# Four array quarters for the backward direction and a turned T in the RWKV chunk stages

## The chip, the core and the metric

The kernel runs on one core of a Trainium2 chip. The metric is the device time of the whole kernel in microseconds, as a median of several runs; less is better. TensorE is called PE here, VectorE DVE, ScalarE ACT, GpSimd POOL.

## What is computed

One trunk layer of a hybrid backbone: 512 latent and 128 context tokens, width 1024. The change touches one part, the RWKV-7 scan in both directions over time, for 8 heads of width 64:

```python
def step(s, inp):
    r_t, w_t, k_t, v_t, kk_t, a_t = inp
    sa = jnp.einsum("bhvk,bhk->bhv", s, -kk_t)
    s = (s * w_t[:, :, None, :] + sa[..., None] * (kk_t * a_t)[:, :, None, :]
         + v_t[..., None] * k_t[:, :, None, :])
    return s, jnp.einsum("bhvk,bhk->bhv", s, r_t)
for d, reverse in enumerate((False, True)):
    ...
    y, s_fin = _wkv7_scan(rh, w, kd, vh, kk, a, s0[:, d].astype(f32), reverse)
```

The rest (modulated norms, input projection, attention, gated merge, MLP) is dense work on PE and is the same in both kernels.

## The kernel before

The scan is done in chunks of 64 tokens (`CH`). Within a chunk the recurrence is a triangular system, so the kernel needs the inverse of a 64 by 64 unit triangular matrix for each chunk, direction and head. It builds that inverse by doubling the solved block size, in levels.

Two heads make a head pair: one head lies in partitions 0 to 63, the other in 64 to 127. The function `chunks(it)` runs twice (`it` 0 and 1), the "half" of the text, and each half works on two head pairs `s` = 0 and 1. A half takes five groups `g`; a group holds, for each pair, two directions `d` and two chunks `q`, so eight 64 by 64 problems of one pair are handled by one "stage". Stages are named by two letters:

- KB and KA (L853): products of bt and of kt with ar, 64 by 128 each. AB and AK on DVE mask them into `abm` and `akm`.
- R0 and T0 (DVE): the first level of the inverse `rm` and its transpose `tm`.
- for levels l = 1 to 5: H_l (PE, L873) multiplies `abm` with `tm`; ACT copies the result from PSUM to `hm` (L1488); G_l (PE, L885) multiplies `hm` with `rm`; C_l (DVE, L1877) copies the blocks of that level into `tm`; V_l (DVE, L1881) transposes `tm` back into `rm`. After G5 comes V5 (L1873), the last copy into `rm`.
- TR (L865): bt and kt turned, copied by ACT to `bkt`.
- P, U, S, Y for q = 0 and 1: right side, solution (`rm` times `pw`), new state, output. ACT copies P and U out, DVE scales the state (S, L1892), ACT or DVE moves Y out. These are LAGGED: in round r they work on group r - 1, while the H and G stages work on group r.

No scheduler is involved. The lists `PE_ST`, `DV_ST` and `AC_ST` are the order of the stages in one round for each engine; `paired` issues each stage for s = 0 and then for s = 1. Each engine works its list strictly in order, and a stage starts with waits on counters of the stages that it needs. In the second half ACT and DVE also have pieces of the next phase between these stages (`between_stages`: splitting the attention output, L1459 and L1916, and a weight block).

A float32 matmul shows in the trace as two records, so one H stage of one pair is 16 records: 2 directions, 2 chunks, 2 heads, 2 records. A matmul of head 0 reads partitions 0 to 63 and writes partitions 0 to 63, one of head 1 reads and writes 64 to 127. This is the matter of the change: of the four quarters of the array (input half by output half) two are used.

## Time and profile before

| | |
|---|---|
| median of 3 runs | 1368.11 us (1368.07 to 1368.47) |
| the profiled execution, its own time | 1369.97 us |
| its span, first to last instruction | 1368.2 us |
| mean granted PE clock | 0.983 |
| PE busy | 1289.2 us, 94% |
| DVE busy | 689.7 us, 50% |
| ACT busy | 550.7 us, 40% |
| first half of the chunk stages | 321.5 to 446.0 us |
| second half | 587.6 to 707.9 us |

Busy time is the union of the records of an engine. A PE record lasts until its result has landed, so that neighbours overlap: a PE that shows as busy can still be waiting for short times between stages.

### The profile page before, as it was taken

To read this page: it belongs to the slowest core of one execution; us is meant where nothing else is said; L and a number is where in the kernel's file an instruction comes from. 1 tells how busy PE (TensorE), PEld (TensorE's weight loads), DVE (VectorE), ACT (ScalarE), POOL (GpSimd) and SP (SyncE) were. 2 spreads that over 40 slices of the span, in tenths; PEclk is the share of its full clock that TensorE was granted. 3 is DMA by queue.
4 is the path that set the end of the run, shared out by engine and by line. 5 is a ranking of instruction groups with operands and counts; after the bars stand their busy time and mean duration, and the time that the engine had idled before them with its cause. 6 is when DMAs were issued, how large, how long until landed. Compare 5 with 4: busy or idle time off the path is not lost.

```text
span 1368.2 us, 31729 instructions
## 1 busy us (share of the span) xinstructions
PE 1289.2 (94%) x13903; PEld 1191.0 (87%) x13903; DVE 689.7 (50%) x1036; ACT 550.7 (40%) x864; POOL 42.2 (3%) x103
## 2 busy tenths in 40 slices
PE   4899999998999779999999999899999999999995
PEld 1899999998999554489989878799999999999995
DVE  3427742642544666565547512554554544533544
ACT  3635534432233577624342212733433334333433
POOL 0100011000010000000000000000000000000000
PEclk9899999999999999999999999999999999999998
DMA  9422265315000200010116495022121121022222
GB/s 389 147 72 101 100 267 183 119 49 210 9 5 4 93 1 1 0 54 4 39 42 230 172 376 185 10 87 89 61 92 61 63 90 38 23 77 73 72 71 93
DMA packets 24027, 131.70 MB, mean 96 GB/s; under 512 B 2896, under 2 KB 3664, under 8 KB 15344
## 3 DMA queue, kind: packets, MB, share of 16 engines
q1 hardware_dynamic: 19104, 103.98, 21.7%
q0 software_dynamic: 4816, 26.11, 5.1%
q8 instruction: 90, 1.47, 0.5%
q14 instruction: 17, 0.14, 0.0%
HBM read 111.74 MB, written 18.34 MB: 95 GB/s over the span
## 4 chain that ended last, share of the span: by engine, by line
PE 58%; DVE 4%; ACT 3%; DMA 1%; issue 1%; DVEq 0%; ACTq 0%
PE ps L715 29%; PE ps L1230 11%; PE ps L885 2%; PE ps L873 2%; PE ps L1096 2%; PE ps L853 1%; PE ps L740 1%; PE ps L759 1%; DMA adl<-in_wada 1%; DVE nmax L1995 1%; PE ps L750 1%; PE ps L1002 1%; PE ps L1072 1%; PE ps L865 1%; PE ps L1043 1%
## 5 line engine op out<-in xcount | busy, mean ns | idle before, releaser
L715 PE MATMUL ps<-h2lo,whi 128*128 128x322 f32 x672 | 154.5, 311 | 0.7 <-ACT facc L1332 0.7
L715 PE MATMUL ps<-h2hi,wlo 128*128 128x322 f32 x672 | 155.0, 312 | 0.0
L715 PE MATMUL ps<-h2hi,whi 128*128 128x322 f32 x672 | 154.0, 310 | 0.0
L1685 DVE TENSOR_TENSOR wlo<-raw,whi 128x2048 fp32r<-128x2048 f32 x47 | 107.5, 2288 | 75.1 <-ACT whi L1293 75.1
L715 PE MATMUL ps<-hlo,whi 128*128 128x322 f32 x544 | 127.9, 316 | 1.0 <-ACT qkv L1358 1.0
L715 PE MATMUL ps<-hhi,wlo 128*128 128x322 f32 x544 | 125.4, 312 | 0.0
L715 PE MATMUL ps<-hhi,whi 128*128 128x322 f32 x544 | 124.7, 310 | 0.0
L715 PEld LDWEIGHTS ps<-h2hi,whi 128*128 128x128 f32 x672 | 114.2, 190 | 0.0
L715 PEld LDWEIGHTS ps<-h2lo,whi 128*128 128x128 f32 x672 | 113.0, 189 | 0.9 <-DVE wlo L1685 0.9
L715 PEld LDWEIGHTS ps<-h2hi,wlo 128*128 128x128 f32 x672 | 113.7, 189 | 0.0
L1732 DVE SCALAR_TENSOR_TENSOR facc<-fraw,par,facc 128x642 f32<-128x642 f32 x44 | 39.0, 887 | 137.3 <-ACT facc L1332 137.3
L1331 ACT ACTIVATE fraw<-ps 128x644 f32<-128x644 f32 x44 | 31.2, 710 | 181.4 <-PE ps L715 180.1
L1293 ACT ACTIVATE whi<-raw 128x2048 fp32r<-128x2048 f32 x47 | 90.0, 1915 | 17.3 <-PE ps L715 11.8
L715 PEld LDWEIGHTS ps<-hlo,whi 128*128 128x128 f32 x544 | 91.4, 189 | 4.2 <-issue 2.4
L715 PEld LDWEIGHTS ps<-hhi,whi 128*128 128x128 f32 x544 | 92.4, 190 | 0.0
L715 PEld LDWEIGHTS ps<-hhi,wlo 128*128 128x128 f32 x544 | 91.9, 189 | 0.0
L1230 PE MATMUL ps<-dlo,whi 128*128 128x322 f32 x344 | 79.3, 312 | 3.2 <-DVE dlo L2149 2.1
L1230 PE MATMUL ps<-dhi,wlo 128*128 128x322 f32 x344 | 79.5, 313 | 0.0
L1230 PE MATMUL ps<-dhi,whi 128*128 128x322 f32 x344 | 78.5, 309 | 0.0
L2148 DVE TENSOR_TENSOR wlo<-raw,whi 128x512 fp32r<-128x512 f32 x44 | 30.4, 692 | 84.2 <-ACT dhi L1631 84.2
L1877 DVE COPY_PREDICATED tm<-con,ps 128x256 f32<-128x256 int32 x80 | 35.6, 445 | 65.9 <-PE ps L885 65.0
L1630 ACT ACTIVATE whi<-raw 128x512 fp32r<-128x512 f32 x44 | 27.8, 633 | 95.0 <-PE ps L1230 93.0
(353 smaller groups left out, 2592.7 us busy)
## 6 DMA issues: line engine op xcount, KB each, us to landing
raw<-in_wblk SPq DMA_DIRECT2D x48, 1024.0 KB, 4.9
adl<-in_wada SPq DMA_DIRECT2D x8, 2048.0 KB, 8.1
raw<-in_wdn SPq DMA_DIRECT2D x44, 256.0 KB, 2.6
adaw<-in_wada SPq DMA_DIRECT2D x4, 2048.0 KB, 20.3
gate_scratch<-gout POOLq DMA_DIRECT2D x16, 322.0 KB, 2.5
gld<-gate_scratch POOLq DMA_DIRECT2D x8, 644.0 KB, 4.6
attention_inputs_used<-attention_scratch SPq DMA_DIRECT2D x1, 5056.0 KB, 15.4
u_scratch<-uout POOLq DMA_DIRECT2D x12, 320.0 KB, 2.4
```

Source lines behind the costliest of these rows:

```text
L715: mm = pe.matmul(o, w, v, start=first, stop=last and w is hi and x is xh[n])
L873: mm = pe.matmul(bank(b1, CH, CH * (2 * d + q))[r], abm[s][g % 2][r, d, q, 0, :], tm[s][r, d, q, :], start=True, stop=True)
L885: mm = pe.matmul(bank(b0, CH, CH * (2 * d + q))[r], left, right, start=True, stop=True)
L1096: mm = pe.matmul(bank(4 + u % 2)[64 * p:64 * p + 64], vo_u[:, c, u // 2, 64:128], pt[p][:, c, :], start=c == 0, stop=c == 5)
L1230: mm = pe.matmul(o, w, v, start=(k == 0 and q == 0), stop=(k == FF - 1 and q == 2))
L1293: ac.activation(whi[s][:, :], raw[s][:, :], ACT.Copy).then_inc(hi_done, 1)
L1331: ac.activation(fr[j][:, :], tile(2 * j), ACT.Copy)
L1630: ac.activation(whi[0][:, 512:1024] if second else whi[s][:, 0:512], raw[s][:, 0:512], ACT.Copy)
L1685: TT(wlo[s][:, :], raw[s][:, :], whi[s][:, :].bitcast(F32), ALU.subtract).then_inc(lo_done, 1)
L1732: st.last(STT(fa[j][:, 1:TP - 1], fr[j][:, 0:TP - 2], taps(0), fa[j][:, 1:TP - 1], ALU.mult, ALU.add))
L1877: ins = dv.copy_predicated(t1[:, :, :, :], lev[:, l - 1].unsqueeze(2).broadcast_to(each), steps_of(bank(b0, 4 * CH)))
L2148: TT(wl, raw[s][:, 0:512], wh.bitcast(F32), ALU.subtract)
```

## The change

Five things are done. (1) The backward direction (d = 1) writes its products H, P and U into the other half of the output partitions (`away`), and reads them there in G and U; so d = 0 uses two quarters of the array and d = 1 the other two. The two directions write to two PSUM banks, and ACT and DVE read two banks in one instruction. (2) H now also multiplies `tm` with the identity, which turns it; ACT copies both results to `hr`, and G takes both operands from there. V1 to V4 on DVE go; T0 and the V5 copy stay. H5 turns T into `rm` with an ACT copy of its own. (3) KA moves from behind KB to the end of the round, AK with it. (4) The lists of stages are written anew. (5) PE gets its stages from `staggered`: pair 0 runs one stage ahead of pair 1. DVE and ACT keep `paired`.

```diff
@@ -322,16 +323,15 @@
             for s in range(2):
                 made[s].insert(0, sb(f"{name}{s}_{g}", [P, 2, 2, 2, CH]))
         if g:
-            tm = [sb(f"tm{s}", [P, 2, 2, CH]) for s in range(2)]
-            hm = [sb(f"hm{s}", [P, 2, 2, CH]) for s in range(2)]
+            hr = [sb(f"hr{s}", [P, 2, 2, 2, CH]) for s in range(2)]
             assert spot[0] == ring_half
...
-    PE_ST = ["KB", "KA", "P0", "H1", "U0", "G1", "S0", "Y0", "H2", "G2", "P1", "H3", "U1", "G3", "S1", "Y1", "H4", "G4",
-             "TR", "H5", "G5"]
-    DV_ST = ["AB", "R0", "T0", "AK", "C1", "V1", "S0", "C2", "V2", "C3", "V3", "S1", "Y1", "C4", "V4", "V5"]
-    AC_ST = ["P0", "H1", "U0", "H2", "P1", "H3", "U1", "Y1", "H4", "TR", "H5"]
+    PE_ST = ["KB", "P0", "U0", "S0", "H1", "Y0", "G1", "H2", "P1", "G2", "U1", "H3", "S1", "G3", "H4", "Y1", "G4", "H5", "TR",
+             "G5", "KA"]
+    DV_ST = ["AB", "R0", "T0", "S0", "C1", "C2", "S1", "C3", "Y1", "C4", "V5", "AK"]
+    AC_ST = ["P0", "U0", "H1", "H2", "P1", "U1", "H3", "H4", "Y1", "H5", "TR"]
...
+    def staggered(names):
+
+        stages = list(in_order(names))
+        first = [(g, name, 0) for g, name in stages]
+        second = [(g, name, 1) for g, name in stages]
+        out = [first[0], second[0], first[1]]
+        for a, b in zip(first[2:], second[1:]):
+            out += [a, b]
+        return out + [second[-1]]
...
             if name in ("KB", "KA"):
-                if g == 0:
+                if name == "KA":
+                    ac("H5")
+                elif g == 0:
                     pe.wait_ge(dv_prep, 10 * it + 10)
-                elif name == "KA":
+                else:
                     dv("V5", g - 1)
-                else:
-                    ac("H5", g - 1)
-                b, src = (b1, bt[s]) if name == "KB" else (b0, kt[s])
+                b, src = (b0, bt[s]) if name == "KB" else (b1, kt[s])
...
             elif name[0] == "H":
                 l = int(name[1])
                 dv("T0" if l == 1 else f"C{l - 1}")
-                for d in range(2):
+                for turn in range(2):
                     for q in range(2):
-                        for r in half:
-                            mm = pe.matmul(bank(b1, CH, CH * (2 * d + q))[r], abm[s][g % 2][r, d, q, 0, :], tm[s][r, d, q, :],
-                                           start=True, stop=True)
+                        for d in range(2):
+                            for r, away in zip(half, half[::-1]):
+                                left, right = (tm[s][r, d, q, :], ident[r, r]) if turn else \
+                                    (abm[s][g % 2][r, d, q, 0, :], tm[s][r, d, q, :])
+                                mm = pe.matmul(bank(b0 + d, CH, CH * (2 * turn + q))[away if d else r], left, right,
+                                               start=True, stop=True)
             elif name[0] == "G":
                 l = int(name[1])
                 ac(f"H{l}")
-                dv("AK" if l == 1 else f"V{l - 1}")
-                for d in range(2):
-                    for q in range(2):
-                        for r in half:
-                            left, right = rm[s][g % 2][r, d, q, :], hm[s][r, d, q, :]
+                for q in range(2):
+                    for d in range(2):
+                        for r, away in zip(half, half[::-1]):
+                            at = away if d else r
                             if l == 5:
-                                left, right = right, left
-                            mm = pe.matmul(bank(b0, CH, CH * (2 * d + q))[r], left, right, start=True, stop=True)
+                                mm = pe.matmul(bank(b0, CH, 4 * CH + CH * (2 * d + q))[at], hr[s][at, d, 0, q, :],
+                                               rm[s][g % 2][at, d, q, :], start=True, stop=True)
+                            else:
+                                mm = pe.matmul(bank(b0 + d, CH, 4 * CH + CH * q)[r], hr[s][at, d, 1, q, :],
+                                               hr[s][at, d, 0, q, :], start=True, stop=True)
             elif name[0] == "P":
                 if q == 0:
                     ac("TR")
+                    dv("AK")
+                    if g > 0:
+                        if g - 1 in ADDED:
+                            dv("Y1", g - 1)
+                        else:
+                            ac("Y1", g - 1)
                     if g == 1:
                         pe.wait_ge(sl_done, it + 1)
                     elif g > 1:
                         dv("S1", g - 1)
                 else:
                     dv("S0")
-                for d in range(2):
-                    for r in half:
-                        mm = pe.matmul(bank(b2, CH, CH * d)[r], akm[s][g % 2][r, d, q, 0, :], vt64[s][r, chunk_of(g, d, q), :],
-                                       start=True, stop=first)
-                    if not first:
-                        for r in half:
-                            mm = pe.matmul(bank(b2, CH, CH * d)[r], ar[s][r, d, chunk_of(g, d, q), 0, :], state(q)[r, d, :],
-                                           start=False, stop=True)
+                    if g == NG - 1:
+                        pe.wait_ge(pe_g[s], at_stage(PE_ST, it, g, "Y0"))
+                for n in range(1 if first else 2):
+                    for d in range(2):
+                        for r, away in zip(half, half[::-1]):
+                            left, right = (ar[s][r, d, chunk_of(g, d, q), 0, :], state(q)[r, d, :]) if n else \
+                                (akm[s][g % 2][r, d, q, 0, :], vt64[s][r, chunk_of(g, d, q), :])
+                            mm = pe.matmul(bank(b2 + d, CH, 6 * CH)[away if d else r], left, right, start=n == 0,
+                                           stop=first or n == 1)
...
                 for d in range(2):
-                    for r in half:
-                        mm = pe.matmul(bank(b2, CH, P + CH * d)[r], rm[s][g % 2][r, d, q, :], pw[s][r, d, :], start=True, stop=True)
+                    for r, away in zip(half, half[::-1]):
+                        at = away if d else r
+                        mm = pe.matmul(bank(b2 + d, CH, 7 * CH)[r], rm[s][g % 2][at, d, q, :], pw[s][at, d, :], start=True,
+                                       stop=True)
...
-                if q == 0 and g > 0:
-                    if g - 1 in ADDED:
-                        dv("Y1", g - 1)
-                    else:
-                        ac("Y1", g - 1)
...
-            for g, name, s in paired(PE_ST):
+            for g, name, s in staggered(PE_ST):
...
                 if name[0] == "H":
-                    ins = ac.activation(hm[s][:, :, :, :].rearrange("p d q n -> p (d q n)"), bank(b1, 4 * CH), ACT.Copy)
+                    if name == "H5":
+                        ac.activation(hr[s][:, :, 0, :, :].rearrange("p d q n -> p d (q n)"), ps[:, b0:b0 + 2, 0:2 * CH], ACT.Copy)
+                        ins = ac.activation(rm[s][g % 2][:, :, :, :].rearrange("p d q n -> p d (q n)"),
+                                            ps[:, b0:b0 + 2, 2 * CH:4 * CH], ACT.Copy)
+                    else:
+                        ins = ac.activation(hr[s][:, :, :, :, :].rearrange("p d m q n -> p d (m q n)"),
+                                            ps[:, b0:b0 + 2, 0:4 * CH], ACT.Copy)
                 elif name[0] in "PU":
-                    dst, at = (pw[s], 0) if name[0] == "P" else (uw[s], P)
-                    ins = ac.activation(dst[:, :, :].rearrange("p d n -> p (d n)"), bank(b2, P, at), ACT.Copy)
+                    dst, at = (pw[s], 6 * CH) if name[0] == "P" else (uw[s], 7 * CH)
+                    ins = ac.activation(dst[:, :, :], ps[:, b2:b2 + 2, at:at + CH], ACT.Copy)
...
-                ins = dv.copy_predicated(r1[:, :, :, :], last.unsqueeze(2).broadcast_to(each), steps_of(bank(b0, 4 * CH)))
+                ins = dv.copy_predicated(r1[:, :, :, :], last.unsqueeze(2).broadcast_to(each), steps_of(bank(b0, 4 * CH, 4 * CH)))
...
-                ins = dv.copy_predicated(t1[:, :, :, :], lev[:, l - 1].unsqueeze(2).broadcast_to(each), steps_of(bank(b0, 4 * CH)))
-            elif name == "T0" or name[0] == "V":
-                mine("R0" if name == "T0" else "C" + name[1])
-                src, dst = (r1, t1) if name == "T0" else (t1, r1)
-                ins = dv.transpose(dst[:, :, :, :].rearrange("p d q n -> p (d q n)"), src[:, :, :, :].rearrange("p d q n -> p (d q n)"))
+                ins = dv.copy_predicated(t1[:, :, :, :], lev[:, l - 1].unsqueeze(2).broadcast_to(each),
+                                         ps[:, b0:b0 + 2, 4 * CH:6 * CH].rearrange("p d (q n) -> p d q n", q=2))
+            elif name == "T0":
+                mine("R0")
+                ins = dv.transpose(t1[:, :, :, :].rearrange("p d q n -> p (d q n)"), r1[:, :, :, :].rearrange("p d q n -> p (d q n)"))
...
-            if name in ("V2", "V4") and 1 <= g <= 3:
-                lows(2 * g - 2 + (name == "V4"))
+            if name in ("C2", "C4") and 1 <= g <= 3:
+                lows(2 * g - 2 + (name == "C4"))
```

On PE, first where the third level meets the state stage, in the middle of a round. L909 is U, L885 is G, L916 to L920 are S; buffers 191 and 192 belong to pair 0 and pair 1. Before:

```order
L909 MATMUL ps<-pw_191,rm_0_185 64x64 x4
L909 MATMUL ps<-pw_192,rm_0_187 64x64 x4
L885 MATMUL ps<-hm_177,rm_1_186 64x64 x8
L885 MATMUL ps<-hm_178,rm_1_188 64x64 x8
L916 MATMUL ps<-si_1_196,con 64x64 x2
L918 MATMUL ps<-vt_0_189,bkt_0_183 64x64 x2
L920 MATMUL ps<-uw_193,bkt_0_183 64x64 x2
```

Of the change (L886 is H with its turn, L899 is G, L940 to L944 are S, hr_177 is pair 0, tm_190 pair 1):

```order
L886 MATMUL ps<-tm_190,abm_0_182 64x64 x8
L886 MATMUL ps<-con,tm_190 64x64 x8
L899 MATMUL ps<-hr_177 64x64 x8
L940 MATMUL ps<-si_1_200,con 64x64 x2
L942 MATMUL ps<-vt_1_192,bkt_1_176 64x64 x2
L944 MATMUL ps<-uw_196,bkt_1_176 64x64 x2
...
L886 MATMUL ps<-tm_189,abm_0_181 64x64 x8
L886 MATMUL ps<-con,tm_189 64x64 x8
```

Before, G3 of both pairs is followed by S1 of both; now S1 of pair 1 stands behind G3 of pair 0.

The same place on DVE. L1877 is C, L1881 is V, L1892 is the scaling of the state (si_0_195 of pair 0, si_0_197 of pair 1). Before, C3, V3, the state of q = 1, C4:

```order
L1877 COPY_PREDICATED tm_175<-con,ps 128x256
L1877 COPY_PREDICATED tm_176<-con,ps 128x256
L1881 STREAM_TRANSPOSE rm_0_185<-tm_175 128x256
L1881 STREAM_TRANSPOSE rm_0_187<-tm_176 128x256
L1892 TENSOR_TENSOR si_0_195<-ps,ex_144 128x128
L1892 TENSOR_TENSOR si_0_197<-ps,ex_145 128x128
L1877 COPY_PREDICATED tm_175<-con,ps 128x256
L1877 COPY_PREDICATED tm_176<-con,ps 128x256
```

Of the change (L1902 is C, L1917 the state), from C2 to C4:

```order
L1902 COPY_PREDICATED tm_189<-con,ps 128x256
L1902 COPY_PREDICATED tm_190<-con,ps 128x256
L1917 TENSOR_TENSOR si_0_197<-ps,ex_144 128x128
L1917 TENSOR_TENSOR si_0_199<-ps,ex_145 128x128
L1902 COPY_PREDICATED tm_189<-con,ps 128x256
L1902 COPY_PREDICATED tm_190<-con,ps 128x256
L1902 COPY_PREDICATED tm_189<-con,ps 128x256
L1902 COPY_PREDICATED tm_190<-con,ps 128x256
```

The transposes are gone, and the state of both pairs now stands ahead of C3 of pair 0 where it stood behind C3 and V3.

## Rows read from the trace of the kernel before

**Rows 1.** Head of the page: the span.

```profile
span 1368.2 us, 31729 instructions
```

**Rows 2.** Windows: us, then PE, PEld, DVE, ACT, POOL busy, PEclk, DMA, GB/s.

```profile
321.50:343.20 21.70, 17.89 (x449) 16.33 (x450) 10.52 (x25) 5.74 (x13) 2.02 (x5) 0.96 0.88 316
...
587.60:604.60 17.00, 16.63 (x455) 15.29 (x450) 10.27 (x25) 5.63 (x13) 1.38 (x4) 1.00 0.21 86
604.60:627.10 22.50, 22.44 (x696) 22.03 (x694) 13.97 (x37) 8.70 (x26) 0.75 (x2) 1.00 0.02 4
627.10:650.90 23.80, 23.75 (x742) 23.34 (x740) 13.46 (x35) 8.97 (x26) 0.75 (x2) 1.00 0.05 9
650.90:676.00 25.10, 24.01 (x745) 23.46 (x742) 13.41 (x33) 8.79 (x24) 0.75 (x2) 1.00 0.13 46
676.00:707.90 31.90, 31.79 (x983) 30.85 (x979) 15.53 (x38) 10.87 (x30) 0.10 (x1) 1.00 0.02 5
```

**Rows 3.** Groups of PE instructions by form in 587.6 to 707.9.

```profile
L873 PE MATMUL ps<-tm,abm 64*64 64x64 f32 x800 | 27.8, 219 | 0.3
L885 PE MATMUL ps<-hm,rm 64*64 64x64 f32 x640 | 22.6, 220 | 0.2
...
L897 PE MATMUL ps<-vt,akm 64*64 64x64 f32 x160 | 9.7, 218 | 1.0 <-issue 1.0
...
L853 PE MATMUL ps<-ar,bt 64*64 64x128 f32 x160 | 9.6, 269 | 0.0
...
L901 PE MATMUL ps<-si,ar 64*64 64x64 f32 x128 | 8.0, 218 | 0.0
L909 PE MATMUL ps<-pw,rm 64*64 64x64 f32 x160 | 6.9, 220 | 0.0
L885 PE MATMUL ps<-rm,hm 64*64 64x64 f32 x160 | 5.7, 221 | 0.2
```

**Rows 4.** Timeline of one level, all engines.

```profile
384.18 1.10 PE L873 MATMUL ps<-tm,abm 64*64 64x64 f32 x32
...
384.86 0.85 ACT L1488 ACTIVATE hm<-ps 128x256 f32<-128x256 f32 x2
...
385.29 1.15 PE L885 MATMUL ps<-hm,rm 64*64 64x64 f32 x32
386.02 0.91 DVE L1877 COPY_PREDICATED tm<-con,ps 128x256 f32<-128x256 int32 x2 [2.74 <-PE ps L885]
...
386.27 0.28 PE L865 MATMUL ps<-con,bt 64*64 64x64 f32 x4
```

**Rows 5.** Groups of ACT and of DVE by form, 587.6 to 707.9.

```profile
L1488 ACT ACTIVATE hm<-ps 128x256 f32<-128x256 f32 x50 | 19.2, 384 | 30.7 <-PE ps L873 28.5
L1493 ACT ACTIVATE bkt<-ps 128x512 f32<-128x512 f32 x10 | 6.0, 597 | 8.2 <-PE ps L865 8.2
L1491 ACT ACTIVATE pw<-ps 128x128 f32<-128x128 f32 x20 | 5.5, 278 | 28.1 <-PE ps L901 23.6 <-PE ps L897 4.5
...
L1459 ACT ACTIVATE branch_hi<-raw 128x512 fp32r<-128x512 f32 x4 | 2.5, 623 | 0.0
...
L1877 DVE COPY_PREDICATED tm<-con,ps 128x256 f32<-128x256 int32 x40 | 17.8, 445 | 31.9 <-PE ps L885 31.4
L1881 DVE STREAM_TRANSPOSE rm<-tm 128x256 f32<-128x256 f32 x40 | 15.3, 420 | 0.0
...
L1892 DVE TENSOR_TENSOR si<-ps,ex 128x128 f32<-128x128 f32 x14 | 3.8, 275 | 3.3 <-PE ps L920 2.5
```

**Rows 6.** Modulation blocks, four column groups: by form; one whole; its first four.

```profile
L750 PE MATMUL ps<-adl,silu_c 128*32 128x512 f32 x128 | 15.4, 598 | 1.6 <-DMA adl<-in_wada 1.6
...
781.56 1.92 PE L750 MATMUL ps<-adl,silu_c 128*32 128x512 f32 x16
...
781.56 0.64 PE L750 MATMUL ps<-adl,silu_c 128*32 128x512 f32 x4
```

**Rows 7.** Timeline of PE behind a gap, then a window behind it.

```profile
340.45 1.03 PE L873 MATMUL ps<-tm,abm 64*64 64x64 f32 x28 [2.67 <-issue]
...
341.40:344.90 3.50, 3.48 (x52) 3.41 (x50) 0.89 (x2) 0.43 (x2) 0.00 (x0) 0.51 0.11 30
```

More of the change, by code:

```diff
@@ L301, in build @@
     stv = [w[:, 3 * P:4 * P].rearrange("p (d n) -> p d n", d=2) for w in hpw]
+    smid = [sb(f"smid{s}", [P, 2, CH]) for s in range(2)]
     assert spot[0] <= keep_u, (spot[0], keep_u)
@@ L329, in build @@
         rm[s] += [sb(f"rm{s}_{g}", [P, 2, 2, CH]) for g in range(2)]
+    tm = [sb(f"tm{s}", [P, 2, 2, CH]) for s in range(2)]
     vt64 = [sb(f"vt64_{s}", [P, NC, CH]) for s in range(2)]
@@ L333, in build @@
     si = [[sb(f"si{s}_{n}", [P, 2, CH]) for n in range(2)] for s in range(2)]
-    smid = [sb(f"smid{s}", [P, 2, CH]) for s in range(2)]
     ysum = [sb(f"ysum{s}", [P, NT, P]) for s in range(2)]
@@ L1863, in chunk_stage @@
             if name in ("AB", "AK"):
-                b, dst = (b1, abm[s]) if name == "AB" else (b0, akm[s])
+                b, dst = (b0, abm[s]) if name == "AB" else (b1, akm[s])
                 product("KB" if name == "AB" else "KA")
@@ L1869, in chunk_stage @@
                 dv.wait_ge(po_g[s], at_stage(PO_ST, it, g, "R0"))
-                ins = dv.copy_predicated(r1[:, :, :, :], near.unsqueeze(2).broadcast_to(each), steps_of(bank(b1))[:, :, :, 0:CH])
+                ins = dv.copy_predicated(r1[:, :, :, :], near.unsqueeze(2).broadcast_to(each), steps_of(bank(b0))[:, :, :, 0:CH])
             elif name == "V5":
                 product("G5")
-                ins = dv.copy_predicated(r1[:, :, :, :], last.unsqueeze(2).broadcast_to(each), steps_of(bank(b0, 4 * CH)))
+                ins = dv.copy_predicated(r1[:, :, :, :], last.unsqueeze(2).broadcast_to(each), steps_of(bank(b0, 4 * CH, 4 * CH)))
             elif name[0] == "C":
```

## Prediction

> **What bounds the kernel now.** I read the windows first. The chunk stages take 321.5 to 446.0 us and 587.6 to 707.9 us; nothing that the diff touches lies elsewhere, so of the span of 1368.2 us [rows 1] some 245 us are in play. In the windows of the second half, cut at each KB, PE is busy in nearly all of every round: 17.0, 22.5, 23.8, 25.1 and 31.9 us, the fourth with a PE gap of 1.1 us; DVE has 10 to 15 us of work in them and ACT 6 to 11 [rows 2]. A PE record outlives its place in the queue, so "busy" has to be turned into a pace. In the timeline of a level the 32 records of an H stage of both pairs last 1.10 us, of which 0.22 is the last record's way out, so a record takes 0.029 us of PE's time and an H stage of one pair 0.47; the G stages take the same [rows 3, 4]. The 64x128 products take 9.6 us for 160 with five such tails, so 0.056 each [rows 3]. A half has 3264 records of the first kind (H 800, G 800, P 304, U 160, and TR, S and Y, which stay) and 320 of the second: 95.0 + 17.9 = 112.9 us of work. The second half takes 120.3 us, so PE waits some 7.4 us in it, the gap included. PE's work is the bound, and the waits are small.
>
> The same timeline gives the delays from engine to engine. H starts at 384.18, its first copy on ACT at 384.86, that is 0.47 for the stage and 0.21 behind it; the copies end so that G starts at 385.29, 0.05 behind the first of them; C follows at 386.02, again 0.21 behind the G stage when 0.05 for the restart of PE are counted [rows 4].
>
> **What the quarters give.** H gets twice the records (1600), four at a time instead of two. G1 to G4 (640 records), P (304) and U (160) keep their number and go four at a time; G5, KB, KA, TR, S and Y are as before. If four quarters run at once, four records take the 0.058 us of two. H then costs what it did, G saves 640 x 0.0146 = 9.3 us, P 4.4, U 2.3: 16.0 us a half.
>
> No row of this trace shows four 64x64 quarters. The nearest one are the modulation blocks, where the output is cut into four column groups: 128 records of 598 ns take 15.4 us in all, a block of 16 takes 1.92 us, and its first four lie within 0.64 us, so they start within 0.04 us of each other [rows 6]. So four parts of the array work at once and four starts are no obstacle; I take four. The bound from the other side is no gain at all over two (the pace of rows 3): H costs 23.3 us more a half, the others as before.
>
> The Trainium skill says otherwise: "TensorE: Matmul & The Clock Gate", in the section on the gap of 56 ns, has a floor of about 25 ns from start to start, however small the matmul. The trace speaks against it, by the four starts within 0.04 us [rows 6]. By the skill's floor a quarter's record would cost 0.025 us, and the 2704 of them in a half 28 us more than I take: the rival "few quarters" below.
>
> **What the new order costs.** I walk each round through the three lists with these durations: H 0.47 a pair, G 0.23, U 0.12, P 0.23; ACT's copy of H has 512 columns instead of 256, so 0.60 (the bkt copy) instead of 0.38; P and U copies 0.28, C 0.445, state 0.275 [rows 5]; an engine's next instruction can start some 0.09 before the last one's end. A stage starts when its queue has come to it and its inputs are there. Waits of PE in one half:
>
> - First round, nothing lagged. Before, a level takes 0.47 + 0.21 + 0.38 + 0.10 + 0.47 + 0.21 + 0.445 + 0.10 = 2.4 us. Now the copy is 0.22 longer and G 0.23 shorter: 2.4 again, with less work in it. PE waits 6.5 us (2.5 before).
> - Each of the four rounds with lagged work: S0 of pair 0 waits 0.80, because ACT takes P0 of both pairs before U0 of pair 0, and PE now issues P0 of pair 1 behind U0 of pair 0. H2 of pair 1 waits 0.55 for G1 and C1. U1 of pair 0 waits 0.66, the same crossing on ACT. H4 of pair 0 waits 0.96: on DVE the state of pair 1 now stands ahead of C3 of pair 0, and on PE S1 of pair 1 stands behind G3 of pair 0. Small ones 0.4. Together 3.4 us a round (0.8 before), 13.6 for four.
> - DVE adds the output of groups 0 and 3 (Y1) ahead of C4: 1.5 and 1.1 us before H5; and 0.8 in small waits in the second round.
> - The last round's lagged stages alone: AK now comes at the end, P0 waits 1.35 and 0.88 for it, S0 0.80, Y1 0.80 and 0.61: 4.4 us (1.1 before).
>
> That is 6.5 + 13.6 + 3.4 + 4.4 = 27.9 us against 7.3 us when the kernel before is walked in the same way (112.9 + 7.3 = 120.2; the trace has 120.3). So the first half changes by 27.9 - 7.3 - 16.0 = +4.6 us. In the second half ACT splits the attention output behind H2 and H4 of pair 1, 0.62 + 0.30 us [rows 5] or 0.73; before, this lay in ACT's idle time. Now P1's copy is queued behind it and U1 waits for that: 0.84, 0.84 and 0.64 more, and H5 0.7 more: +3.0. Second half +7.6 us.
>
> The V transposes (40 of 0.42 us a half [rows 5]) I cost at nothing: DVE is not what PE waits for there, G had its `rm` before ACT had `hm`. The buffer moves cost nothing either; no wait changes by them.
>
> **Sum.** 4.6 + 7.6 = +12.2 us, on the profiled execution (1368.2 us of span, 1.8 of time around it, 1369.97) and so on the median of 1368.1: 1380.3. PE's waits make one more half-speed window in the first rounds likely: there is one now, at 341.4 us, granted 0.51, behind a gap of 2.67 us in which PE waited for no engine [rows 7]; that round takes 21.7 us instead of 17.0 [rows 2]. PE will be at work for 12.0 of 18.5 us in a first round. I add 1 us for it. Predicted: 1381 us.
>
> **The rivals.**
>
> 1. The crossings overlap (faster). The four large waits of a lagged round (0.80, 0.55, 0.66, 0.96 = 3.0 us) rest on exact places in three queues; eight rounds hold 24 us. If they all vanish because the stages ahead of them finish a little sooner, the time is 1357. It decides at half of them, 12 us. For it: DVE loses 40 transposes of 0.42 us a half [rows 5], so its queue is emptier than the walk's worst places need. Against it: each is a queue's order, not a load, and each stage behind it is 0.23 to 0.6 long.
> 2. Few quarters (slower). With no more than two at once, the work is 136.2 us a half and the waits mostly disappear in it: about 160 a half, 1447 us. Rows 6 speak against it. An estimate by the Trainium skill's floor (the page named above), 125 us of work a half, would give about 150 a half and 1428 us.
> 3. Clock and instructions (slower). Every first round and every last round falls to the lower of PE's two levels, 1.2 instead of 2.4 GHz, for part of its length. The one case in the trace cost at most the 4.7 us by which the two first rounds differ, a gap of PE's own in it [rows 2, 7]; three more such would give 1381 + 14 = 1395. A half also has 3200 more PE instructions of 0.0146 us or less, so gaps "issue" like those at 340.45 would come more often.
> 4. No change: the waits grow by just what the quarters give, 1368.
>
> **How the numbers follow.** The forecast (with partly overlapping waits, 1372 to 1392) has a chance of 0.6; rival 1 0.17, spread from 1350 to 1367; rival 2 0.07; rival 3 0.12; no change 0.04. A measurement of this kernel tells about 0.2% (2.7 us) from no change. Faster by more: 0.18 (rival 1 and a little of the rest); within: 0.05; slower: 0.77. The range leaves out rival 2 and the ends of rivals 1 and 3: 1357 to 1399.
>
> **What would show it.** In the profile of the changed kernel: H with its turn should take 0.47 us a pair (32 records that last 0.7), G 16 records in some 0.45 with its tail; if H takes 0.93 the quarters don't overlap. Rounds from KB to KB of about 18.5, 24.2, 23.3, 23.3 us, and PE's busy share falling in them. ACT's H copy at 0.60. In the waits of PE, H on tm (DVE) and U and S on pw and uw (ACT) should lead, where now they hardly appear. Wrong would make me: H waits for C3 that don't come up because the state stage of pair 1 is done in time; or a last tail much shorter than 4 us.

## The result

The changed kernel takes 1417.35 us (median of 4 runs, 1414.47 to 1419.82) against 1368.29 for the kernel before beside it: 1.0348 times as long, 95% interval 1.0317 to 1.038. The forecast was 1381 us with a range of 1357 to 1399. The sign was right, the loss (49 us) four times as large as forecast (13), and outside the range.

The page of the changed kernel: the span, TensorE's busy time, and the queue that brings instructions (packets, MB).

```profile
span 1415.6 us, 34777 instructions
...
PE 1277.8 (90%) x15503; PEld 1171.3 (83%) x15503; DVE 662.7 (47%) x956; ACT 570.9 (40%) x884; POOL 43.4 (3%) x103
...
q8 instruction: 102, 1.67, 0.5%
```

The windows, cut at each KB as in [rows 2], with the first half above and the second below.

```profile
321.60:348.70 27.10, 17.15 (x595) 15.48 (x596) 6.71 (x15) 7.89 (x15) 2.01 (x5) 0.87 0.71 254
348.70:374.70 26.00, 21.62 (x854) 19.97 (x849) 9.68 (x24) 9.41 (x24) 0.80 (x2) 1.00 0.03 9
374.70:401.90 27.20, 22.55 (x902) 21.07 (x900) 9.19 (x22) 9.62 (x24) 0.80 (x2) 1.00 0.02 5
401.90:429.60 27.70, 22.52 (x907) 21.04 (x905) 9.21 (x22) 9.62 (x24) 4.34 (x4) 1.00 0.02 5
429.60:468.00 38.40, 30.10 (x1156) 27.96 (x1152) 12.66 (x30) 10.96 (x30) 0.00 (x0) 1.00 0.02 4
611.10:630.80 19.70, 15.02 (x597) 13.13 (x595) 6.72 (x15) 7.78 (x15) 1.33 (x4) 1.00 0.18 74
630.80:656.70 25.90, 21.02 (x856) 19.71 (x853) 11.26 (x28) 10.72 (x28) 1.07 (x2) 1.00 0.01 4
656.70:683.20 26.50, 22.29 (x903) 21.23 (x899) 10.87 (x26) 10.85 (x28) 1.07 (x2) 1.00 0.12 34
683.20:714.90 31.70, 24.03 (x906) 22.81 (x902) 10.72 (x24) 10.71 (x26) 1.21 (x2) 0.95 0.05 16
714.90:756.50 41.60, 32.33 (x1167) 29.18 (x1163) 15.00 (x33) 12.85 (x32) 1.06 (x2) 1.00 0.06 15
```

From the first record of the first KB to the start of the last record of Y, the halves take 146.4 and 143.2 us (124.4 and 120.2 before): +22.0 and +23.0, together nearly all of the 49. The excess over the forecast lies in every round and not in one accident: 27.1, 26.0, 27.2, 27.7 and 38.4 us in the first half, where 18.5, 24.2, 23.3 and 23.3 were forecast and some 35.5 were left for the last (120.2 + 4.6, less the four). The granted clock is 1.00 in eight of the ten windows (0.87 and 0.95 in the others), so it isn't the clock either. TensorE is busy for 22 of 27 us in a middle round, and idle in a kernel that it was said to bound.

What it waits for, in the waits of PE over the chunk stages of the second half (us in total, times, longest):

```profile
PE ps L886 <- DVE tm L1902: 6.8, 10, 1.7
PE ps L923 <- issue: 4.7, 6, 1.2
PE ps L886 <- issue: 3.5, 4, 1.5
PE ps L863 <- issue: 2.3, 1, 2.3
PE ps L940 <- ACT uw L1516: 2.3, 4, 0.6
PE ps L886 <- DVE tm L1906: 2.2, 2, 1.8
PE ps L875 <- issue: 2.2, 3, 1.1
PE ps L899 <- ACT hr L1512: 1.6, 4, 0.7
```

L886 is H, L923 P, L863 KB and KA, L940 the state, L899 G, L875 TR; L1902 is C and L1906 T0 on DVE. Half of the list is what the prediction had named: H on `tm`, the state on `uw`. The other half is "issue", TensorE idle while nothing that the profile shows holds it. All such rows of this view sum to 16.4 us in the first half and 14.9 in the second; in the kernel before they sum to 3.5 and 1.0. The view counts a halt from the modelled end of the last record, about 0.2 us behind its start, so it understates each. Not every such row is a halt without a cause: of the first half's 16.4 us, 1.9 are the two stages P0 of the last round (L923), which the new order makes wait for AK.

Where the halts fall is the finding. TensorE's timeline of the changed kernel, first around 407 us, then around 409 and 413:

```profile
406.90 0.46 PE L886 MATMUL ps<-tm,abm 64*64 64x64 f32 x16
407.18 0.41 PE L886 MATMUL ps<-con,tm 64*64 64x64 f32 x16
...
409.01 0.33 PE L886 MATMUL ps<-con,tm 64*64 64x64 f32 x7
409.54 0.34 PE L886 MATMUL ps<-con,tm 64*64 64x64 f32 x8 [0.20 <-issue]
...
412.18 0.46 PE L886 MATMUL ps<-tm,abm 64*64 64x64 f32 x16 [0.33 <-DVE tm L1902]
413.26 0.46 PE L886 MATMUL ps<-con,tm 64*64 64x64 f32 x16 [0.63 <-issue]
```

The first two rows are H and its turn as forecast: 16 records in 0.28 us, the next 16 about as fast, 0.47 us to the next stage's start. The stages at 409 and 413 break off inside, in the middle of the turn or between product and turn, where no instruction carries a wait. Counting TensorE's instructions (a record of a matmul and a record of a weight load are one each) gives their places. Below, worked out from the trace of the changed kernel, is each transfer of the instruction queue and each longer halt from 407 to 428 us that the profile calls "issue", with the number of instructions that PE had started by then. The first three halts lie inside a stage, the last three between two stages:

```
transfer 407.19 took 0.96
halt     409.12 -> 409.54  0.41   after instruction  9086
transfer 410.65 took 1.32
halt     412.42 -> 413.26  0.84   after instruction  9342
transfer 414.38 took 0.96
halt     416.01 -> 416.72  0.71   after instruction  9598
transfer 417.86 took 1.30
halt     420.02 -> 420.45  0.43   after instruction  9854
transfer 421.70 took 1.16
halt     423.12 -> 424.45  1.33   after instruction 10110
transfer 425.48 took 1.21
halt     427.48 -> 428.18  0.70   after instruction 10366
```

The numbers differ by exactly 256. The queue moved 1.67 MB in 102 packets, 16 KB each. The kernel before, with 3200 TensorE instructions fewer, has 90 packets, and a run with 6144 more than that (e4 below) has 114: 24 packets for 24 x 256 instructions. So a packet is a block of 256 instructions; TensorE runs out at the end of a block and goes on, in this stretch, 2.3 to 2.8 us after a transfer began. (The Trainium skill, "Advanced Engine Details and Errata", section on the ISA cache, has a line of 16 KB, 256 instructions. The halts and the packets agree. How many lines TensorE holds, no run here shows.) The changed kernel issues 8768 TensorE instructions in a half, the one before 7168.

The place can be followed through whole traces. When the semaphore instructions of PE's own sequencer, which are records too, are counted with the others, the numbers of all these halts leave the same remainder, 193, when divided by 256. In the halves of every run below, each "issue" halt of over 0.3 us from start to start is one of them, other than the stages P0 of the last round (the wait for AK) and a single one in e9. So the time lost at block ends can be summed for each run. The table has this in us for the two halves together (a halt is a step of over 0.1 us from one start to the next, less the 0.03 us of a usual one). "Rest" is the halves' time without it, "walked" what the prediction's way of walking the stages, which knows no supply, gave against before.

| run | halves | at block ends (halts) | rest | rest against before | walked |
|---|---|---|---|---|---|
| before | 244.5 | 5.2 (5) | 239.3 | | |
| changed | 289.6 | 36.2 (45) | 253.4 | +14.1 | +12.2 |
| e1, more instructions | 277.6 | 25.5 (40) | 252.1 | +12.8 | |
| e7, more small ones | 278.1 | 26.4 (38) | 251.7 | +12.4 | |
| e3, no turn | 246.7 | 7.6 (12) | 239.2 | -0.1 | -5 |
| e10, half of the turn | 273.9 | 23.2 (32) | 250.7 | +11.4 | |
| e2, pairs together | 281.7 | 42.3 (51) | 239.4 | +0.1 | -2 |
| e11, e10 and e2 | 257.0 | 22.3 (33) | 234.7 | -4.6 | |
| e9, lag alone | 275.0 | 2.7 (5) | 272.3 | +33.0 | +32 |
| e6, quarters alone | 235.9 | 14.7 (25) | 221.2 | -18.1 | -19 |
| e5, two quarters | 323.4 | 4.5 (3) | 318.9 | +79.6 | +79 |
| e8, state once | 267.8 | 3.9 (5) | 263.9 | +24.6 | |

Of the 45 us that the two halves grew, 31 are halts at block ends, and the other 14 are about what the walk forecast. A halt and a wait for a queue can cover each other, so this is a split of what the trace shows and not a proof that the two add.

### The profile page after: what moved, and what is told of

Its sections match the earlier page's. It is cut to its first block, busy times and chain, and to the rows that moved or that the text cites. A ratio compares the mean times of both kernels' runs of the same rounds, so it can differ in the third digit from the quotient of the medians.

```text
span 1415.6 us, 34777 instructions
## 1 busy us (share of the span) xinstructions
PE 1277.8 (90%) x15503; PEld 1171.3 (83%) x15503; DVE 662.7 (47%) x956; ACT 570.9 (40%) x884; POOL 43.4 (3%) x103
## 3 DMA queue, kind: packets, MB, share of 16 engines
q8 instruction: 102, 1.67, 0.5%
## 4 chain that ended last, share of the span: by engine, by line
PE 55%; DVE 4%; ACT 3%; issue 2%; DMA 1%; DVEq 0%; ACTq 0%
PE ps L725 28%; PE ps L1249 10%; PE ps L886 2%; PE ps L1115 2%; PE ps L863 1%; PE ps L750 1%; PE ps L769 1%; DMA adl<-in_wada 1%; DVE nmax L2020 1%; PE ps L760 1%; PE ps L1021 1%; PE ps L899 1%; PE ps L1091 1%; PE ps L875 1%; PE ps L1092 1%
## 5 line engine op out<-in xcount | busy, mean ns | idle before, releaser
L725 PE MATMUL ps<-hlo,whi 128*128 128x322 f32 x544 | 127.9, 316 | 1.0 <-ACT qkv L1377 1.0
L1512 ACT ACTIVATE hr<-ps 128x512 f32<-128x512 f32 x80 | 47.6, 597 | 91.9 <-PE ps L886 91.9
L1902 DVE COPY_PREDICATED tm<-con,ps 128x256 f32<-128x256 int32 x80 | 35.3, 442 | 88.6 <-PE ps L899 88.6
## 6 DMA issues: line engine op xcount, KB each, us to landing
attention_inputs_used<-attention_scratch SPq DMA_DIRECT2D x1, 5056.0 KB, 15.5
```

Source lines behind the costliest of these rows:

```text
L725: mm = pe.matmul(o, w, v, start=first, stop=last and w is hi and x is xh[n])
L1512: ins = ac.activation(hr[s][:, :, :, :, :].rearrange("p d m q n -> p d (m q n)"), ps[:, b0:b0 + 2, 0:4 * CH], ACT.Copy)
L1902: ins = dv.copy_predicated(t1[:, :, :, :], lev[:, l - 1].unsqueeze(2).broadcast_to(each), ps[:, b0:b0 + 2, 4 * CH:6 * CH].rearrange("p d ( ...
```

## The experiments

Theory F: TensorE's instruction supply is the bound; a block of 256 instructions costs a least time, and the 1600 instructions more per half (the turn) are what costs. Theory Q: the places in the queues, above all the lag of pair 0, cost more than walked. Theory K: the clock. Each run was made beside runs of the kernel before, whose medians were 1369.7 (e1 to e4), 1369.3 (e5 to e8) and 1370.1 us (e9 to e11).

**e1, more instructions and nothing else.** In the H stages of the kernel before:

```diff
                             mm = pe.matmul(bank(b1, CH, CH * (2 * d + q))[r], abm[s][g % 2][r, d, q, 0, :], tm[s][r, d, q, :],
                                            start=True, stop=True)
+                        for r, away in list(zip(half, half[::-1])) * (0, 2, 1, 1, 1)[l - 1]:
+                            mm = pe.matmul(bank(b0, CH, 4 * CH + CH * (2 * d + q))[away], abm[s][g % 2][r, d, q, 0, :],
+                                           tm[s][r, d, q, :], start=True, stop=True)
```

> The kernel before with 400 more 64x64 matmuls per half (8 for each H stage: none in H1, 16 in H2, 8 in H3 to H5), which repeat the stage's operands into the other two quarters of the array and unused columns of PSUM. Nothing reads them, so the output is unchanged. They run beside the real ones (four starts within 20 ns in the trace after), so they add no time of the array, no wait and no work to any other engine; they add 1600 TensorE instructions to 7168 per half. Theory F (instruction supply: TensorE gets 256 instructions per fetch, one fetch per 3.4 to 3.7 us at best): 34 fetches per half instead of 28, at 3.7 us 127 us and more, with halts inside stages at each boundary of 256: 5 to 15 us more per half, the kernel at 1380 to 1398 us. Theory Q (the queue crossings of the staggered order are what costs): no change, 1368 us, since the order is that of before. Theory K (TensorE's clock): no loss either, TensorE does more.

Measured: 1405.97 us, ratio 1.026 (1.0224 to 1.0296), +36 us. Neither the order nor a wait differs from before. Q and K don't give this; F does for the larger part: halts at block ends grew by 20 us. The rest is array time, which the expectation had put at nothing: in H2, with 16 added matmuls for a pair, the records of both pairs take 1.87 us from the first start to the last where they took 0.88, and in H3 to H5, with 8 added, 0.99: 13 us in all.

**e7, the same number of instructions with an eighth of the columns.** As e1 with `bank(b0, 8, ...)` and `tm[s][r, d, q, 0:8]`.

> As e1, but the added matmuls have 8 columns instead of 64. If the 36 us of e1 came from the array (work or power), an eighth of the columns gives most of them back: 1370 to 1380 us. Theory F: the instruction count is the same, so the time is that of e1: 1400 to 1410 us.

Measured: 1401.95 us, ratio 1.0239 (1.0204 to 1.0275). The 4 us between e7 and e1 lie within the two intervals: an eighth of the columns gives nothing back. The halts at block ends are the same (26.4 and 25.5 us), as the number of instructions is. H2 still takes 1.84 us, so the 13 us of stage time isn't a matter of columns either; what sets it was not tried.

**e4, the supply by itself.** Ahead of the second half of the kernel before, where PE alone works:

```diff
+        for n in range(512):
+            r, c = (slice(64 * (k % 2), 64 * (k % 2) + 64) for k in (n, n // 2))
+            mm = pe.matmul(bank(3 if r == c else 7, 64, 64 * (n // 4 % 8))[c], ident[r, r], ident[r, 0:64], start=True, stop=True)
...
+            mm = pe.matmul(bank(3 if r == c else 7, 8, 64 * (n // 4 % 8))[c], ident[r, r], ident[r, 0:8], start=True, stop=True)
...
+            r = slice(64 * (n % 2), 64 * (n % 2) + 64)
+            mm = pe.matmul(bank(3, 64, 64 * (n // 2 % 8))[r], ident[r, r], ident[r, 0:64], start=True, stop=True)
```

> The kernel before with three blocks of 512 more fp32 matmuls between the attention phase and the second half, where no other engine works for the result; nothing reads what they write. Each block is 2048 TensorE instructions, eight fetches. Block 1: 64x64 tiles in all four quarters, 64 columns: 15 us by the array's pace (58.3 ns for four). Block 2: the same with 8 columns: below 8 us by the array. Block 3: two quarters, 64 columns: 30 us by the pace of before. Theory F: blocks 1 and 2 take the same, 27 to 30 us each (eight fetches of 3.4 to 3.7 us), block 3 about 30 us; together 84 to 90 us, the kernel at 1452 to 1458 us. Without a limit of supply: 15, 8 and 30 us, the kernel at 1421 us.

Measured: 1461.74 us, ratio 1.0662 (1.0632 to 1.0692), +92 us. Its PE timeline, one row for each stretch without a halt (a matmul's record x128 and its weight load's make the 256):

```profile
584.16 4.07 PE L1144 MATMUL ps<-con 64*64 64x64 f32 x263 [2.15 <-DVEq L486]
592.54 3.49 PE L1144 MATMUL ps<-con 64*64 64x64 f32 x128 [4.30 <-issue]
596.26 2.09 PE L1144 MATMUL ps<-con 64*64 64x64 f32 x128 [0.24 <-issue]
599.72 2.09 PE L1144 MATMUL ps<-con 64*64 64x64 f32 x128 [1.36 <-issue]
603.72 2.09 PE L1144 MATMUL ps<-con 64*64 64x64 f32 x128 [1.91 <-issue]
607.73 2.09 PE L1144 MATMUL ps<-con 64*64 64x64 f32 x128 [1.91 <-issue]
611.73 1.98 PE L1144 MATMUL ps<-con 64*64 64x64 f32 x121 [1.91 <-issue]
...
645.37 32.55 PE L1156 MATMUL ps<-con 64*64 64x64 f32 x1024
```

With four quarters the array does 128 records in 1.9 us (2.09 with the way out) and then stands for up to as long again. From 592.54 to 613.80 DVE, ACT and GpSimd do nothing and the DMA engines are busy for 0.02 of the time. The starts are 3.72, 3.46, and then three times 4.00 us apart. So 4.00 isn't a least time: over blocks 1 and 2 the 13 steps from a halted block to the next run from 3.46 to 4.02 us, 3.80 in the mean, and in the changed kernel, the first rounds' long ones left out, 29 such steps run from 3.45 to 4.02, 3.75 in the mean. The table of halts from 407 to 428 us has five of them, 3.72, 3.46, 3.73, 4.00 and 3.73. Block 3, at the pace of two quarters, runs 1024 records with no halt; six of its blocks in a row take 3.73 us each, which is the array's own pace, and supply keeps up. The windows of the three blocks:

```profile
584.16:613.80 29.64, 17.91 (x1025) 16.93 (x1025) 0.49 (x2) 0.00 (x0) 3.37 (x30) 0.94 0.17 62
613.80:645.37 31.57, 27.95 (x1025) 27.23 (x1025) 0.00 (x0) 0.00 (x0) 0.00 (x0) 0.55 0.02 4
645.37:677.99 32.62, 32.55 (x1024) 32.41 (x1025) 0.00 (x0) 0.00 (x0) 0.00 (x0) 0.92 0.02 4
```

Work of the array that differs by a factor of two and more takes 29.6, 31.6 and 32.6 us. The second block ran at a granted clock of 0.55, most of it at 1.2 GHz, and the third at 0.92, so 31.6 and 32.6 us are no clean readings of 256 instructions; the steps above are.

**e3, the turn left out.** What the kernel leaves out is the turn, so its output isn't the right one. In the changed kernel `for turn in range(1)`, with `ident` in place of the turned T in G1 to G4, and H5's second copy taken from the product.

> The changed kernel without the turn: the second eight matmuls of each H stage are left out, G takes a constant matrix instead of the turned T, so the output isn't the reference's; all other stages, copies and the order stay. TensorE issues 7168 instructions per half again. The walk of the stages, in which the turn costs 0.23 us per stage of array time and no instruction supply exists, gives 115.7 and 119.4 us per half, which is 9 us less per half than the same walk for the changed kernel: 1408 us. Theory F: the 1600 instructions come with six fetches and their halts, so each half loses these 9 us and 12 to 18 us of halts: 1364 to 1382 us. Theory Q: only the 9 us per half: 1395 to 1408 us.

Measured: 1374.22 us, ratio 1.0034 (1.002 to 1.0049): 43 us below the changed kernel, where the array's time alone gave 9 us a half, 18 together (the 1408 of the expectation counted them once). The two halves take 124.5 and 122.3 us. The halts at block ends fall from 36.2 to 7.6 us, the rest by 14.

**e10, half of the turn given back to VectorE.**

```diff
-                        for d in range(2):
+                        for d in range(turn, 2):
...
+                if l > 1:
+                    dv(f"V{l - 1}")
...
+                mine("C" + name[1])
+                ins = dv.transpose(r1[:, 0, :, :].rearrange("p q n -> p (q n)"), t1[:, 0, :, :].rearrange("p q n -> p (q n)"))
```

> The changed kernel with half of the turn given back to VectorE: for direction 0, whose product stays on its own partitions, T is turned by a half-sized transpose on VectorE after each C stage, and the four turn matmuls of each H stage are left out; same result. TensorE issues 7968 instructions per half instead of 8768. Theory F: 31.1 fetches of 4.0 us in place of 34.3, 12.5 us less per half: 1392 us (1386 to 1400). By array time and crossings alone the four matmuls are worth 0.12 us per stage, 5 us per half: 1407 us or more, since VectorE gets eight more stages a round.

Measured: 1399.66 us, ratio 1.0216 (1.0191 to 1.024). The 1600 instructions fewer (both halves) bring 17.7 us where F expected 25; just within its bounds, and more than the 10 that array time gave. With e3 this makes a row of three: 8768, 7968 and 7168 instructions a half, 1417.4, 1399.7 and 1374.2 us, 11 and 16 ns for an instruction, array time included; the halts at block ends are 36.2, 23.2 and 7.6 us.

**e2, the lag undone.** In the changed kernel:

```diff
-            for g, name, s in staggered(PE_ST):
+            for g, name, s in paired(PE_ST):
```

> The changed kernel with one edit undone: TensorE issues each stage for both pairs in turn again (paired order), all else as changed. Theory Q: the lag of pair 0 is what costs, so most of the 49 us come back; the walk of the stages gives 118.0 and 120.5 us per half against 120.2 before, the kernel at 1366 us. Theory F: the 8768 instructions per half stay, so the halts inside stages stay: each half 15 to 22 us above the walk, the kernel at 1400 to 1412 us. Theory K as F with the clock below 0.95 in the rounds.

Measured: 1409.0 us, ratio 1.0299 (1.0262 to 1.0336). The lag is worth 8 us of the 49 and Q is out as the main cause. Without the halts e2 would be 14 us below the changed kernel, which is what the walk says; 6 of them go into more halts at block ends. The "issue" rows sum to 17.7 and 15.0 us in its halves.

**e11, both.** e10's edit in e2's order.

> As e10, with both pairs' stages issued in turn again as in e2. Theory F: the same 12.5 us less per half than e2: 1384 us (1377 to 1393), still slower than the kernel before. By array time alone 1399 us or more.

Measured: 1387.91 us, ratio 1.0142 (1.0112 to 1.0171), 21 us below e2. It computes the right output, is the fastest version of the changed kernel here that does, and is still slower than the kernel before.

**e9, the lag alone.** The kernel before with `staggered(PE_ST)`.

> The kernel before with one part of the change alone: TensorE issues the first head pair one stage ahead of the second; lists, quarters, transposes and result stay those of before, 7168 TensorE instructions per half. The stages' walk gives 136.4 us per half against 120.2 (the products now wait for copies and transposes that run for both pairs in turn): the kernel at 1400 us. Theory F adds nothing here, since 256 instructions have 4.9 us at that pace: 1395 to 1405 us, with few halts inside stages. If lagging costs less than walked (crossings overlap), 1368 to 1390 us.

Measured: 1403.51 us, ratio 1.024 (1.0213 to 1.0267), +33 us where the walk gave 32. Its waits of PE in the second half are queue places and nothing else (L895 is G there, L883 H, and L1891 the transposes of T0 and of V):

```profile
PE ps L895 <- ACT hm L1498: 7.0, 8, 1.0
PE ps L883 <- DVE tm L1891: 3.0, 5, 0.9
PE ps L895 <- DVE rm L1891: 2.9, 3, 1.0
```

No "issue" row of size is among them (0.0 us in the half): at 134.9 us for 7168 instructions a block has 4.8 us. So the walk of the queues was sound, and halts go away when TensorE asks for less.

**e6, the quarters alone.** In the kernel before, H2 to H5 and G2 to G4:

```diff
+                            out = bank(b1, CH, CH * (2 * d + q))[r] if l == 1 else bank(b0 + d, CH, 4 * CH + CH * q)[at]
+                            mm = pe.matmul(out, abm[s][g % 2][r, d, q, 0, :], tm[s][r, d, q, :], start=True, stop=True)
```

> The kernel before with four quarters at work in H2 to H5 and G2 to G4 and nothing else: each matmul of the backward direction writes to the other head's partitions and G reads there; the turned T isn't there, so the output isn't the reference's. Instructions (7168 per half), order, copies and transposes are those of before. Array work per half falls by 16.3 us; the walk of the stages without a limit of supply gives 110.5 us per half against 120.2: the kernel at 1349 us. Theory F: 28 fetches per half at 3.75 to 4.0 us are 105 to 112 us, and what waits are not hidden (7 us) come on top: 112 to 119 us per half, the kernel at 1354 to 1366 us, with halts at boundaries of 256 instructions that the kernel before didn't have.

Measured: 1362.42 us, ratio 0.9948 (0.9928 to 0.9967). The walk without supply said 20 us faster; 7 came. (For the backward direction G reads the `rm` of the other head here, so the output isn't the right one.) Halts at block ends grew by 9.5 us; without them the halves would be 18 us shorter than before. They are in its waits of the second half (L888 is G, L900 P, L919 the state; 4.5 us of "issue" in all, 5.6 in the first, against 1.0 and 3.5 before):

```profile
PE ps L888 <- ACT hm L1494: 3.9, 11, 0.5
PE ps L919 <- issue: 1.0, 2, 0.8
PE ps L900 <- issue: 0.9, 1, 0.9
```

**e5, the changed kernel in two quarters.** `half` in place of `half[::-1]` in H, G, P and U.

> The changed kernel with every tile kept in the two quarters of its own rows (no tile crosses to the other head's partitions); the same 8768 TensorE instructions per half, the same order, copies and result. If four quarters had worked no better than two, this would be no slower than the changed kernel, 1417 us. By the pace of two quarters (29 ns a record) the stages' walk gives 158.4 and 161.2 us per half, the kernel at 1447 us. Theory F: at that pace 256 instructions take 3.75 us, which the block 3 of the supply run (e4) got without a halt, so the halts nearly vanish and the walk holds: 1442 to 1456 us, 25 to 39 us over the changed kernel. Theory Q (crossings cost more than walked): the same excess as in the changed kernel on top of the walk, 1480 us or more.

Measured: 1450.09 us, ratio 1.0586 (1.0561 to 1.0612). So the four quarters do work, and they bring the changed kernel 33 us; by the walk (158.4 and 161.2 against 125 and 128 us a half) they would have brought 66. The table has the other half: without the halts at block ends the two kernels are 65.5 us apart, and supply takes 31.7 of them back.

**e8, fewer instructions by a larger tile.** In the state stages of the kernel before:

```diff
-                        for r in half:
-                            pe.matmul(out[r], ident[r, r], state(q)[r, d, :], start=True, stop=False)
+                        pe.matmul(out, ident, state(q)[:, d, :], start=True, stop=False)
```

> The kernel before with the state's two 64x64 matmuls by the identity in each S stage made one 128x128 matmul: 144 TensorE instructions fewer per half, the same result. The array's time for them stays (two records of the full array in place of four of 29 ns, about 58 ns each). Without a limit of supply: no change, 1368 us. Theory F: at 14.6 ns an instruction up to 2 us less per half where TensorE's supply binds: 1364 to 1369 us. A tile size that changes within a stage may cost a pause of the array: then 1370 to 1378 us.

Measured: 1395.32 us, ratio 1.0178 (1.0152 to 1.0204), +26 us, above even the third case of the expectation. The count fell by 128 a half. Its timeline:

```profile
633.31 0.46 PE L885 MATMUL ps<-hm,rm 64*64 64x64 f32 x10
633.70 0.43 PE L915 MATMUL ps<-smid,con 128*128 128x64 f32 x2
634.06 0.33 PE L917 MATMUL ps<-vt,bkt 64*64 64x64 f32 x4
634.23 0.28 PE L919 MATMUL ps<-uw,bkt 64*64 64x64 f32 x4
634.44 0.43 PE L915 MATMUL ps<-smid,con 128*128 128x64 f32 x2
```

The last 64x64 record ahead of the large tile starts at 633.55, the first one behind it at 634.06: 0.51 us for two records, where four small ones take 0.12. That is 0.4 us for going to the other tile size and back, and 64 such places are 25 us, the loss. Supply has no part in it: the halts at block ends are 3.9 us, against 5.2 before.

## Why the prediction was wrong

**What held.** Four quarters at once: H with its turn takes 0.47 us a pair as forecast, a record goes every 14.6 ns. The rule that the prediction weighed (the Trainium skill, "TensorE: Matmul & The Clock Gate", a floor of about 25 ns from start to start) doesn't hold here for tiles in different quarters; four 64x64 records start within 20 ns of each other, and 128 of them take 1.87 us (e4), 58 ns for four. ACT's copy of `hr` takes 0.60. The queue crossings were rightly placed and priced, from one matmul record to the next: the state of pair 0 waits 0.79 us at 405.15 (0.80 forecast), H4 0.95 to 0.96 (0.96), the last P0 1.36 and 0.94 (1.35 and 0.88), the last Y1 0.77 (0.80). e9 puts the same walk to the test with a change of its own: 32 us forecast, 33 measured.

**What failed** is the first step, "TensorE's work is the bound, 0.029 us a record", and all sums that stand on it. A record of 0.029 us was read as the time of two quarters of the array. It is also, with its weight load, two instructions at 14.6 ns, 3.7 us for 256, and just there lies the limit of supply (3.45 to 4.02 us a block once it binds). So in its dense stages the kernel before sat at two bounds at once, and its trace shows mostly the one that the reader looked for. So the term "the quarters give 16.0 us a half" was right for the array and wrong for the kernel: with it gone, the supply is next, at once (e6: 7 us instead of 20), and the turn, costed at nothing since "H costs what it did", brought 1600 instructions a half into the resource that had no room. The term that was missing measured 31 us: halts at block ends of 36.2 us in place of 5.2, on top of a walk that came within 2 us (within 1 in e9 and e5, 5 off in e3). It can be seen coming from a count: 8768 / 256 = 34.2 blocks at the mean of 3.75 us are 128 us a half, as much as the whole half by the walk (125 and 128), so that a half has no room for a wait in which no instruction is used. Measured 146.4 and 143.2. That supply doesn't catch up in the waits for queues fits these numbers but was not tried by itself. The price of a block wasn't in the trace of before as such, but the pace of its blocks and the gap at 340.45 marked "issue" were.

**Rival 3** named the kind ("gaps issue would come more often") and priced none of it; it also took 3200 instructions more for a half, when that is both halves together (31006 records in the trace against 27806). Its own figure, so many instructions of 0.0146 us, would have given 23 us a half for the true 1600, and 22 and 23 were lost. That would have been luck: by the table only 15.5 us a half are supply, the rest is the new order, which the sum had already. It wasn't put in the sum, since the gap at 340.45 [rows 7] was read as an accident that may recur.

**Of the loss of 49 us**: not additive, since a halt of supply and a wait for a queue cover each other. Alone, the added matmuls cost 36 (e1; 20 at block ends and 13 of array time) and the lag 33 (e9); the quarters bring 33 in the changed kernel (e5). Taking out of the changed kernel the turn gives 43 back (e3), the lag 8 (e2). With four quarters TensorE is late by supply in any order, so that an order that was walked at 14 us in the changed kernel (118.0 and 120.5 against 124.9 and 127.9 a half) shows 8.

**Open.** What sets the 3.45 to 4.02 us of a block is not settled: in block 1 of e4 a transfer begins 1.0 to 1.6 us behind the restart and PE goes on 2.4 to 3.0 us after it began; what makes it begin no earlier, and why most steps are near 3.46, 3.73 or 4.00 us, no run tells. The long halts of the first rounds are of the same kind: in the changed kernel 4.33 us from 337.95 on, with the transfer begun only at 339.45, in a round where other transfers hold 0.71 of the DMA engines. That those delay it was not tried. This one and the one at 331.75 (2.42 us) are 6.7 us, in a round that takes 8.6 us more than forecast.

## What to carry to other kernels

Count instructions as a resource of their own. For small fp32 tiles a matmul here is four instructions (512 of them make the 2048 of a block in e4), and TensorE, starved, got 256 for each 3.45 to 4.02 us. At that rate, 13.5 to 15.7 ns an instruction, what makes the array faster brings less than its array time (7 us of 20 in e6, 33 of 66 in e5), and a matmul added "beside" others costs its instructions. Before taking an engine's pace for its work, compute it per instruction, and look for "issue" rows that lie a fixed number of instructions apart, some of them inside a stage. What helped here was fewer instructions: half of the turn given to an engine that waits (e10, e11). Fewer by a larger tile lost 26 us, by the change of tile size (e8). Longer moving operands would be another way, which no run tried.

## What the runs showed that I had not expected

- Instructions come 256 at a time (16 KB); TensorE, starved, starts a new block every 3.46 to 4.00 us with 1.9 us of work in it (block 1 of e4); the transfer itself takes 0.9 to 1.4 us. In all traces the halts fall on one place modulo 256.
- Matmuls of 8 columns cost a kernel as much as those of 64 (1402.0 and 1406.0 us, e7 and e1) when 800 of them are added beside the others.
- Four 64x64 fp32 quarters run at once: 128 records in 1.87 us (e4), where two quarters need twice as long.
- A 128x128 matmul of 64 columns between 64x64 ones costs 0.4 us for the two changes of tile size (e8).
